# A four-branch decoder step on one core: the masked tiles of the recurrence move to other buffers, and the wait for GpSimd moves with them

## The reference

```
cols = x @ w_in                                   # one projection, cut into four groups
y_a  = sparse attention over top-128 keys         # A
y_b  = RWKV-7 delta-rule recurrence, normed, gated  # B
y_c  = bg * conv3(cg * xin)                       # C, gated short convolution
y_d  = RG-LRU scan * gelu(gate)                   # D
x = LN(alpha*x + concat(y_a, y_b, y_c, y_d) @ w_out)
x = LN(alpha*x + moe(x))                          # 16 experts, top 2
```

```
sa = s @ a_t
s  = s * w_t + sa * b_t + v_t * k_t
y  = s @ r_t
y  = (y - mean) * rsqrt(var + eps) * g + b        # per head, after the whole scan
```

## Time and profile before

| | us |
|---|---|
| median of 3 runs | 1572.59 (1572.27 to 1572.98) |
| profiled execution, whole | 1574.14 |
| its span, first to last instruction | 1572.5 |
| PE busy | 1249.3 (79%) |
| DVE busy | 675.3 (43%) |
| ACT busy | 342.5 (22%) |
| POOL busy | 163.7 (10%) |

### The profile page before, as it was taken

How to read it: one execution, slowest core, us unless ns; L and a number is a source line. 1 busy time by engine, 2 the same in 40 slices (tenths; PEclk the granted TensorE clock), 3 DMA queues, 4 the chain that set the end, 5 groups by cost and what they waited for, 6 DMA issues and landing times.

```text
span 1572.5 us, 22256 instructions
## 1 busy us (share of the span) xinstructions
PE 1249.3 (79%) x8296; PEld 780.3 (50%) x8296; DVE 675.3 (43%) x1379; ACT 342.5 (22%) x798; POOL 163.7 (10%) x224
## 2 busy tenths in 40 slices
PE   5989996975897198999399899968678925999960
PEld 2566776943444144444156677868344522444420
DVE  0035996866144201111363469977642341111108
ACT  1134231213222011111133422211322211111110
POOL 0030025013000200000201000520210011000011
PEclk9988998986798599999699799989789957999985
DMA  6094111016530358888812021200437014888853
GB/s 243 21 396 185 64 45 44 4 53 174 193 135 1 140 199 315 333 327 344 301 48 74 14 67 54 68 5 4 130 113 311 0 41 160 332 328 329 329 202 138
DMA packets 67918, 246.30 MB, mean 157 GB/s; under 512 B 8723, under 2 KB 29363, under 8 KB 58675
## 3 DMA queue, kind: packets, MB, share of 16 engines
q1 hardware_dynamic: 48736, 177.17, 30.6%
q0 software_dynamic: 14048, 50.00, 8.9%
q10 hardware_dynamic: 5042, 17.90, 2.8%
HBM read 194.39 MB, written 52.87 MB: 157 GB/s over the span
## 4 chain that ended last, share of the span: by engine, by line
PE 52%; issue 21%; DVE 7%; DMA 6%; POOL 4%; ACT 3%; POOLq 3%; SPq 3%; DVEq 2%; ACTq 0%
PE ps L1203 13%; PE ps L805 9%; PE ps L1220 7%; PE ps L1166 7%; PE ps L652 7%; DMA arena<-in_w_dn 2%; SPq L447 1%; POOLq L523 1%; PE ps L1040 1%; DMA arena<-in_wa 1%; POOL rows_in L591 1%; SPq L444 1%; PE ps L1135 1%; DMA arena<-in_wout 1%; DVE arena L2479 1%
## 5 line engine op out<-in xcount | busy, mean ns | idle before, releaser
L1275 ACT ACTIVATE arena<-ps 128x512 f32<-128x512 f32 (+14 forms) x358 | 155.5, 469 | 738.5 <-PE ps L672 162.7
L672 PE MATMUL ps<-arena 128*128 128x272 f32 x1088 | 261.6, 400 | 0.0
L1203 PE MATMUL ps<-arena 128*128 128x512 f32 x512 | 229.8, 601 | 5.9 <-DMA arena<-in_w_dn 3.5
L672 PEld LDWEIGHTS ps<-arena 128*128 128x128 f32 x1088 | 209.2, 194 | 50.8 <-issue 5.5
L805 PE MATMUL ps<-arena 64*64 64x64 f32 (+3 forms) x4016 | 157.4, 240 | 36.3 <-DVE arena L1941 24.2
L805 PEld LDWEIGHTS ps<-arena 64*64 64x64 f32 x4016 | 142.6, 141 | 50.2 <-DVE arena L1941 24.7
L1203 PEld LDWEIGHTS ps<-arena 128*128 128x128 f32 x512 | 97.8, 192 | 132.7 <-issue 132.3
L1220 PE MATMUL ps<-arena 128*128 128x512 f32 x256 | 120.9, 616 | 19.5 <-DVE arena L2479 19.5
L652 PE MATMUL ps<-arena 128*128 128x512 f32 (+1 forms) x256 | 106.0, 574 | 22.2 <-DMA arena<-in_wa 19.0
L2475 DVE TENSOR_TENSOR arena<-arena,ps 128x256 f32<-128x256 f32 x32 | 13.5, 423 | 230.5 <-ACT arena L1593 230.5
L1166 PE MATMUL ps<-arena 128*128 128x512 f32 x256 | 112.4, 594 | 0.0
(11 more groups left out here) (344 smaller groups left out, 1324.5 us busy)
## 6 DMA issues: line engine op xcount, KB each, us to landing
arena<-in_w_gu SPq DMA_DIRECT2D x32, 2048.0 KB, 7.8
arena<-in_w_dn SPq DMA_DIRECT2D x32, 1024.0 KB, 10.8
arena<-in_wf SPq DMA_DIRECT2D x34, 512.0 KB, 3.7
arena<-rows_in SPq DMA_DIRECT2D x32, 512.0 KB, 3.3
rows_out<-arena ACTq DMA_DIRECT2D x32, 512.0 KB, 6.0
rows_in<-arena POOLq DMA_DIRECT2D x12, 1024.0 KB, 24.3
arena<-in_cache_v POOLq DMA_DIRECT2D x64, 128.0 KB, 2.7
arena<-in_cache_k SPq DMA_DIRECT2D x64, 128.0 KB, 2.8
```

The costliest lines, as they stand in the source:

```text
L672: mm = pe.matmul(ps[:, 2 + 2 * h + n % 2, 0:HALF], m.wf[n % 3][:, c, :], m.xT[:, c, h * HALF:h * HALF + HALF], start=c == 0, stop=c == KC - 1)
L1203: mm = pe.matmul(ps[:, 3, :], m.xgT[:, c, :], m.w_gu[k][:, c, :], start=c == 0, stop=c == KC - 1)
L1275: return act.activation(out, in_, ACT.Copy)
```

## The change

Q of group 1, both KM, DT of group 0 and VEb get other addresses. Q of group 1 now lies in LN0 (2048 floats, the whole region), KM of group 0 and DT of group 0 in R1 behind the score buffers (R1B+640 and R1B+1664), KM of group 1 at R4+2048 up to R4+3072, over the weight chunks of the projection. None of them now lies over an fm slot or over tap and conv.

The wait for `fc_used` 2 leaves the head of `rwkv` and stands ahead of `y_centred` on VectorE and ahead of `y_norm` on ScalarE. At the head of `rwkv` VectorE now waits for `zeros_out` and for `ln_done`, since Q of group 1 overwrites LN0. And since LN0 is in use until the recurrence is done, `norm_weights(l, 0)` moves down SyncE's queue, behind the weights of the output projection; it loses its wait for `zeros_out`.

The pieces below are, in order: `memory` (two), `sync_program` behind the load of the recurrent state, `sync_program` behind the load of wout, `y_norm` on ScalarE, `rwkv` on VectorE and `y_centred` on VectorE.

```diff
-    m.Q = [view(at, 8, 4, CH) for at in (R4, R4 + 2048)]
-    m.KM = [view(at, 8, 2, CH) for at in (R4 + 4096, R4 + 5120)]
-    m.DT = [view(at, 8, CH) for at in (R4 + 6144, R1B)]
+    m.Q = [view(at, 8, 4, CH) for at in (R4, LN0)]
+    m.KM = [view(at, 8, 2, CH) for at in (R1B + 640, R4 + 2048)]
+    m.DT = [view(at, 8, CH) for at in (R1B + 1664, R1B)]
...
-    m.VEb = [view(at, DB, CH) for at in (R4 + 6144, R1B)]
+    m.VEb = [view(at, DB, CH) for at in (R1B + 1664, R1B)]
...
-        sp.wait_ge(s["zeros_out"], ZEROED)
-        sp.wait_ge(s["ln_done"], nth(l, "ln_done", 0))
-        sp.wait_ge(s["xt_copied"], nth(l, "xt_copied", 0))
-        norm_weights(l, 0)
...
+        sp.wait_ge(s["ln_done"], nth(l, "ln_done", 0))
+        sp.wait_ge(s["xt_copied"], nth(l, "xt_copied", 0))
+        norm_weights(l, 0)
...
+        act.wait_ge(s["fc_used"], nth(l, "fc_used", 2))
         act.wait_ge(s["yn_mm"], nth(l, "yn_mm", 2))
...
-        dve.wait_ge(s["fc_used"], nth(l, "fc_used", 2))
+        dve.wait_ge(s["zeros_out"], ZEROED)
+        dve.wait_ge(s["ln_done"], nth(l, "ln_done", 0))
         first(0)
...
+        dve.wait_ge(s["fc_used"], nth(l, "fc_used", 2))
         dve.wait_ge(s["rw_a"], nth(l, "rw_a", len(RW_ACT)))
```

## The result

The changed kernel takes 1551.5 us (median, 1550.9 to 1551.9), against 1572.8 us for the kernel before beside it: a ratio of 0.9855, 95% interval 0.9829 to 0.9881. The forecast was 1548.6 with a range of 1543 to 1555, so the sign and the size were right and 2.9 us were missed. The profiled execution took 1550.9 us with a span of 1549.2, against 1574.1 and 1572.5 before: 23.3 us less of span where 24.0 were forecast.

The account below looks back on a forecast made before the run. One wait for GpSimd's convolution at the recurrence's head, for an address, held VectorE and TensorE in each layer. Terms 22.0 (wait) + 2.06 (clock) = 24.0 us, others 0; from 1572.59 to 1548.6 us, range 1543 to 1555.

Parts of the forecast that it names:

- The wait: Head of the recurrence: VectorE starts its masks without waiting for GpSimd, 10.28 + 11.73 = 22.0 us earlier.
- The clock at the squares: TensorE at the recurrence's start: clock stays at 1.00, so VectorE's wait before the second key product goes, 2.06 us.
- upper bound of 3.7: Most the clock term could give: TensorE itself gains 1.8 us a layer at the recurrence's start, 3.7 in all.
- more than the wait can't be won there: Reason for taking 2.06 us: VectorE is busy from the first mask to its wait before the second key product.
- The ports: VectorE's masks beside GpSimd: no cost, as by operands they are like MAX8; upper bound 8.6 us in all.
- the rival's mechanism: Ports rival at the recurrence's head: masks wait for GpSimd one by one, 1551 to 1557 us; chance 0.16.
- The moved wait: Wait for GpSimd moved to y_centred and y_norm: costs nothing, since GpSimd ends long before the norm of y.
- some 60: Cover of the moved wait ahead of the norm of y: some 60 us before lateness would cost in full.
- The norm's weights: Load moved behind the output projection's weights: hidden, cost 0; rival that wout is held up 3.7 us in layer 1, 0.05.
- keep the residual waiting by 3.7 us: Layer 1, SyncE's queue: the 1 MB load delays the residual by 3.7 us, hidden with 1.8 us to spare.
- The clock elsewhere: Rival, sample attention to the prompt's output projection: clock level changes, 5.46 us lost (1554) or as much won (1543).
- The two cases held as rivals to each other: Sample attention: layer 1 falls to layer 0's pace, 1554 us, chance 0.13; or layer 0 rises, 1543 us, 0.12.

Follow-up runs that it names:

- wait_back: Changed kernel with VectorE's wait for both convolution halves put back ahead of the first mask: 1574.8 us against 1576.1 for the kernel before, ratio 0.9987.
- fill_gap: Kernel before plus eleven unused matmuls on TensorE ahead of the recurrence's first products in each layer: 1571.2 us against 1575.6, ratio 0.9969.
- two_op: Changed kernel plus four VectorE instructions with two on-chip operands ahead of the first mask and two behind the second key masks: 1559.5 us.
- pool11: Changed kernel with GpSimd's tap pass over the prompt done eleven times more in the convolution's second half, each layer: 1589.4 us.
- norm_moved: Kernel before with only the first norm's weights loaded behind the output projection's weights: 1575.9 us, ratio 1.0006.
- after_again: The changed kernel itself run once more, beside the kernel before on one chip: 1548.0 us, 27.6 us below the kernel before.

## Why the prediction was right, point by point

**The wait, 22.0 us.** Right: 21.5 came, since 0.26 us a layer stay ahead of the first mask, and wait_back shows that it is this wait. No new wait of any size stands there: TensorE is the releaser in layer 1, by 0.26 us, and zeros and `ln_done` never show as one.

**The clock at the squares, 2.06 us.** Right in mechanism, too small in size: the recurrence gave 4.64, which is above the upper bound of 3.7, too. VectorE's first row of the next steps shows what I left out (before, layer 0 and 1, then after):

```profile
279.20 0.69 DVE L1972 TENSOR_TENSOR arena<-ps,arena 128x512 f32<-128x512 f32 x1 [0.36 <-PE ps L805]
...
1048.28 0.69 DVE L1972 TENSOR_TENSOR arena<-ps,arena 128x512 f32<-128x512 f32 x1 [0.36 <-PE ps L805]
```

```profile
267.56 0.68 DVE L1972 TENSOR_TENSOR arena<-ps,arena 128x512 f32<-128x512 f32 x1
```

From the first mask to the first of these rows of a layer it took 17.64 and 16.74 us before, 15.55 in both layers after: 2.09 and 1.19 us, 3.28 together, of which 2.78 are idle time in such rows: 1.43 and 0.63 at the first wait, 0.36 twice at the second. The step that failed is "more than the wait can't be won there": a second wait, for the eighth powers, came from the same slow start, and I had read only the first. This part lies within the bounds 0 to 3.7, though the upper one was priced with 100 records in 3 us, and the squares hold 84 and 88 in after at 1.00. The other 1.36 us lie nearly all in the recurrence's last steps, which I had taken as rigid: in layer 0 before the clock stood at 0.50 from about 328 to 339, after from about 319 to 326. fill_gap shows the clock's part by itself in layer 0, 3.15 us with the wait left in place, 2.09 of them ahead of the eighth powers.

**The ports, 0.** Right: 6.20 us for twelve masks with GpSimd beside them and without. two_op shows both that the rival's mechanism exists (1.2 us for four instructions with two on-chip operands) and that the masks, with one on-chip operand and one in ps, are not touched by it. MAX8 beside L520 was the right row to go by for them; the slower TENSOR_SCALAR rows of pool11 show that counting operands would not have done for every instruction.

**The moved wait, 0.** Right: the norm of y begins at 332.34 and 1083.63 with 2.60 us idle for TensorE, none for POOL:

```profile
332.34 1.29 DVE L2086 SCALAR_TENSOR_TENSOR arena<-ps,arena 128x512 f32<-128x512 f32 x2 [2.60 <-PE ps L1012]
...
1083.63 1.29 DVE L2086 SCALAR_TENSOR_TENSOR arena<-ps,arena 128x512 f32<-128x512 f32 x2 [2.60 <-PE ps L1012]
```

The cover is 70 us where "some 60" was said, and pool11 shows the price beyond it.

**The norm's weights, 0.** Right: in after wout lands 12.1 and 12.2 us after its issue with the 1 MB behind it (12.0 and 13.4 before, without). DMA issues of layer 0, layer 1's are within 0.1 us:

```profile
arena<-in_wout SPq DMA_DIRECT2D x1, 4096.0 KB, 12.1
...
arena<-in_ln SPq DMA_DIRECT2D x1, 1024.0 KB, 14.0
```

The first load is not held up by the second, as the Trainium skill's "DMA: Bandwidth & Descriptors", section "Two DMAs through the same engine are not ordered", would have it for descriptors that start in order; norm_moved shows it without the rest of the change. That the 1 MB would keep the residual waiting by 3.7 us behind wout was more than it cost: 2.2 us in norm_moved, hidden.

**The clock elsewhere.** The two cases held as rivals to each other, 0.13 and 0.12, both came, one in each layer: 5.22 won and 6.64 lost. The prediction priced both from the earlier trace rows, within 1.2 us; what it did not see is that they could come together and leave the forecast standing. That they nearly cancelled is luck: either one alone would have moved the time by 5 to 7 us. Of the 2.9 us between forecast and median, 2.2 are no stretch at all: the median of after lies 0.6 us above its profiled execution, that of before lay 1.6 below. In the span 0.8 us are missing: 1.4 here, 2.7 in the output projection and the experts, 0.5 at the wait and 0.6 elsewhere, less 2.6 more than forecast in the recurrence and 1.8 in the prompt's attention. So what the recurrence and the prompt's attention gave beyond the forecast paid for what the other stretches lost. That is luck as well, and so is a part of the closeness of the median: the range rested on runs of before within 0.7 us, while later runs of one kernel lay up to 17 us apart.

What stays open: what sets the level of the clock in a given sample attention. It was the same when one kernel ran again (after and after_again), it differed between kernels that reached the stretch at different times, and it went with TensorE's pauses, since filled pauses kept it up in both layers; more the runs don't show.

## What to carry to other kernels

A wait for an address, not for a value, shows as an engine idle for another's last instruction whose result it doesn't read; price it by that idle time, then look for what each engine behind it lost by starting at the lower clock, in every wait that follows and not in the first alone (here the second stood 17 us behind the first mask). Work out the moved wait's cover in us from two rows (the late engine's end, the new waiter's start); within it the wait cost nothing here. Before fearing two engines beside each other, look for rows of the same kind of instruction beside the other engine, with the same operands; the number of on-chip operands alone would have misled for the TENSOR_SCALAR rows of pool11.

## What the hardware did that I had not expected

- The clock fell during single stretches with no change in the work: the same sample attention took 14.8 to 21.6 us in the profiles without added matmuls in it, one output projection group 8.8 us instead of 7.1 (layer 0 of after).
- A pause of 2.08 us ahead of the squares left the clock at 1.00 and one of 2.89 did not; in the sample attention of layer 1 of after it fell about 0.6 us behind the end of one of 2.07.
- Meetings cost GpSimd as well as VectorE: GpSimd's L521 took 2.33 us instead of 1.56 beside VectorE's two-operand work, and in pool11 one of VectorE's last steps (L2065, two on-chip operands) took 1.76 beside GpSimd instead of 0.69.
- A load of 1 MB that follows one of 4 MB on the same queue landed some 2.4 us behind it (14.0 and 12.1 us from two issues 0.5 us apart), where alone it took 6.1.
- The experts' stage, with the same instructions in every kernel here, took 210.1 to 221.5 us in layer 1: a difference as large as the wait that this change removes in a layer.
